# Four column blocks of the first mixing stage computed as two sets of seven block products

## What is computed

```python
h = rmsnorm(x, g_mix[l])
p = h @ w_in[l]                      # 1024 x 5632: F, B, C, V, P (512 each) and three gates of 1024
gates = sigmoid(p[..., OFF_G:]).reshape(b, s, 3, d)
y_f = fourier_mix(p[..., OFF_F:OFF_B], w_fourier[l])
y_c = short_conv(B, C, V, w_conv[l], w_conv_out[l])    # z = C * V, three taps over time, times B, @ w_conv_out
y_p = pool_mix(p[..., OFF_P:OFF_G], w_pool[l], pool_scale[l])
merged = gates[:, :, 0] * y_f + gates[:, :, 1] * y_c + gates[:, :, 2] * y_p
x = x + merged @ w_o[l]
```

## Time and profile before

| | us |
|---|---|
| median of 3 runs (2215.43 to 2217.01) | 2215.58 |
| the profiled execution | 2217.72 |
| its span, first to last instruction | 2215.9 |
| PE busy in the span | 2208.1 |
| DVE busy in the span | 1729.2 |
| ACT busy in the span | 1321.5 |
| mixing stage of the first layer, from about | 188.7 |

### The profile page before, as it was taken

The page is one execution under the profiler, slowest core; times in us unless marked ns, Lnnn a source line. Parts: engine busy times, 40 slices in busy tenths (PEclk is TensorE's granted clock), DMA queues, the critical chain, the costliest instruction groups (busy, mean ns, idle before and its releaser), DMA issues.

```text
span 2215.9 us, 28791 instructions
## 1 busy us (share of the span) xinstructions
PE 2208.1 (100%) x11494; PEld 1886.2 (85%) x11494; DVE 1729.2 (78%) x2163; ACT 1321.5 (60%) x1489; POOL 56.0 (3%) x68
## 2 busy tenths in 40 slices
PE   9999999999999999999999999999999999999999
PEld 8888888888888888888888888888888888788887
DVE  7887566888788566788888799768788887976787
ACT  6566445556556544666656676555565667754555
POOL 0000000000000000000000000000000000000000
PEclk9999999999999999999999999999999999999999
DMA  7977555977879556698597753549778785345876
GB/s 274 327 224 259 166 185 186 310 224 234 287 245 273 187 172 208 215 300 236 193 321 239 236 171 118 204 160 325 231 234 277 239 261 195 105 162 195 287 244 185
DMA packets 170950, 503.86 MB, mean 227 GB/s; under 512 B 18720, under 2 KB 23328, under 8 KB 162624
## 3 DMA queue, kind: packets, MB, share of 16 engines
q1 hardware_dynamic: 161456, 434.90, 55.1%
q0 software_dynamic: 9216, 67.11, 15.4%
q10 hardware_dynamic: 144, 0.00, 0.0%
HBM read 500.91 MB, written 1.05 MB: 227 GB/s over the span
## 4 chain that ended last, share of the span: by engine, by line
PE 90%; DVE 4%; DMA 4%; ACT 1%; issue 1%; SPq 0%; ACTq 0%; DVEq 0%
PE psum L756 24%; PE psum L757 12%; PE psum L692 12%; PE psum L694 12%; PE psum L693 12%; PE psum L888 4%; PE psum L892 4%; PE psum L890 4%; DMA raw<-t_gate_up_1a_dram 2%; DVE split_w L1843 2%; PE psum L724 2%; DMA raw<-t_gate_up_2a_dram 1%; PE psum L1115 1%; DVE gate_up L1983 1%; ACT split_w L1315 0%
## 5 line engine op out<-in xcount | busy, mean ns | idle before, releaser
L1843 DVE TENSOR_TENSOR split_w<-raw,split_w 128x2048 fp32r<-128x2048 f32 (+3 forms) x389 | 842.5, 2177 | 147.4 <-ACT split_w L1315 145.2
L1315 ACT ACTIVATE split_w<-raw 128x2048 fp32r<-128x2048 f32 (+3 forms) x389 | 708.5, 1830 | 291.4 <-PE psum L694 58.4
L756 PE MATMUL psum<-xt,split_w 128*128 128x512 f32 x2464 | 860.1, 393 | 0.5 <-DVE split_w L1843 0.3
L757 PE MATMUL psum<-xt,split_w 128*128 128x256 f32 x2464 | 690.3, 280 | 0.0
L756 PEld LDWEIGHTS psum<-xt,split_w 128*128 128x128 f32 x2464 | 461.2, 187 | 104.0 <-issue 0.6
L757 PEld LDWEIGHTS psum<-xt,split_w 128*128 128x128 f32 x2464 | 465.7, 189 | 0.5
L692 PE MATMUL psum<-split_w,xt 128*128 128x512 f32 (+1 forms) x736 | 289.5, 393 | 0.0
L694 PE MATMUL psum<-split_w,xt 128*128 128x512 f32 (+1 forms) x736 | 283.7, 385 | 0.0
L693 PE MATMUL psum<-split_w,xt 128*128 128x512 f32 (+1 forms) x736 | 283.6, 385 | 0.0
L1983 DVE TENSOR_TENSOR gate_up<-psum,low 128x512 f32<-128x512 f32 x176 | 120.7, 686 | 98.3 <-ACT low L1392 98.1
L692 PEld LDWEIGHTS psum<-split_w,xt 128*128 128x128 f32 x736 | 138.3, 188 | 28.9 <-issue 3.0
(11 more groups left out here) (309 smaller groups left out, 2871.6 us busy)
## 6 DMA issues: line engine op xcount, KB each, us to landing
raw<-w_in_dram SPq DMA_DIRECT2D x180, 512.0 KB, 4.5
raw<-t_gate_up_1b_dram SPq DMA_DIRECT2D x88, 512.0 KB, 6.5
raw<-t_gate_up_2a_dram SPq DMA_DIRECT2D x88, 512.0 KB, 5.9
raw<-t_gate_up_2b_dram SPq DMA_DIRECT2D x88, 512.0 KB, 6.1
raw<-t_gate_up_1a_dram SPq DMA_DIRECT2D x84, 512.0 KB, 6.8
left_sums<-ffn_w_down_quarters_dram POOLq DMA_DIRECT2D x24, 1024.0 KB, 10.0
raw<-ffn_w_down_quarters_dram SPq DMA_DIRECT2D x48, 512.0 KB, 4.4
left_sums<-w_a_quarters_dram POOLq DMA_DIRECT2D x12, 1024.0 KB, 11.0
```

The source lines that it names most:

```text
L756: nc.tensor.matmul(bank, whi[:, slot, w], xt[:, c, :, :], start=c == 0, stop=False)
L757: last = nc.tensor.matmul(bank[:, 0:T], wlo[:, slot, w], xt_hi[:, c, :], start=False, stop=c == DC - 1)
L1315: nc.scalar.activation(whi[:, e.unit(u) % HL, 0:n], raw[:, r, 0:n], ACT.Copy).then_inc(hi_done, 1)
L1843: nc.vector.tensor_tensor(wlo[:, e.unit(u) % HL, 0:n], raw[:, r, 0:n], whi[:, e.unit(u) % HL, 0:n], ALU.subtract).then_inc(w_ready, 1)
```

## The change

The columns C and V are one set (n = 0), and the second halves of the Fourier gate and of the pooling gate are the other (n = 1). For a set, the tokens (two halves) and the depth (even and odd chunks) make the left matrix 2 by 2, and depth and the two column blocks make the right one 2 by 2. In place of two wide products, 96 matmuls, PE computes seven `product`s of 12 matmuls each: 11, U, T2, 21, T3, 22, T4. `w_in_quarters` is a copy of these weights laid out in quarters.

- The sums of token blocks (`s_hi`, `s_lo`, in the space of `mt1`) are made once a layer by `token_sums` and `token_sums_lo` on DVE, with one ACT copy, early in the stage. The three right factors 11, 21 and 22 come through the ring. The four sums come from `set_sums`: POOL issues all their DMAs, the plain loads too. `set_left` holds U, T2 and T4 in turn and `set_right` holds T3, in the space of `poolm`.
- T2 and T3 are added in the bank that holds 11, and 22 in the bank of U. ACT copies the bank away in between (the snapshots `e1`, `u`, `e2`, `e3`), and PE waits for each copy. DVE makes the four output blocks from them (`x00`, `x01`, `x11`, and T4's own bank).
- Order of units now: F, P, B, first half of the Fourier gate, its `t_fourier`, set 0, pooling gate and `w_pool` (n = 0), convolution gate, `w_conv_out`, convolution gate (n = 1), `w_conv_out`, set 1 with `w_pool` inside it ahead of T4, `t_fourier`, `w_o`. There are 38 units, 8 of them sums that do not pass the ring. The merges of the pooling and Fourier branches of n = 1 come after set 1.

```diff
-MIX_UNITS = {1: 32, 2: 36}
+SETS = ({name: 9 + i for i, name in enumerate(("11", "U", "T2", "21", "T3", "22", "T4"))},
+        {"11": 25, "U": 26, "T2": 27, "21": 28, "T3": 29, "22": 30, "T4": 32})
+SET_SUMS = [units[name] for units in SETS for name in ("U", "T2", "T3", "T4")]
+SUMMED = {"U": 0, "T3": 1, "T2": 2, "22": 3}
+MIX_UNITS = {1: 38, 2: 36}
...
+        s_hi, s_lo = (w.rearrange("p (i a) (b t) -> p i (a b) t", a=2, b=2) for w in (mt1_hi, mt1_lo))
...
+        def bank_of(name):
+
+            return 2 if name == "21" else 1 if name in ("U", "22") else 0
...
+                def product(n, name):
+                    out = psum[:, bank_of(name), :]
+                    u = u0 + set_unit(n, name)
+                    slot = e.unit(u) % HL
+                    eng.wait_ge(w_ready, units(e, u, RAW))
+                    for i in range(DC // 2):
+                        hi, lo = left(name, i)
+                        w = slice(i * 512, (i + 1) * 512)
+                        start = i == 0 and name in ("11", "U", "21")
+                        stop = i == DC // 2 - 1
+                        nc.tensor.matmul(out, hi, whi[:, slot, w], start=start, stop=False, skip_group_check=True)
+                        nc.tensor.matmul(out, hi, wlo[:, slot, w], start=False, stop=False, skip_group_check=True)
+                        last = nc.tensor.matmul(out, lo, whi[:, slot, w], start=False, stop=stop, skip_group_check=True)
+                    last.then_inc(w_used, 1)
+
+                wide(u0 + 6, 1, XT)
+                eng.wait_ge(acted, e.after(acted, ("tok", "B")))
+                branch_out(u0 + 8, 2, (fq_hi, fq_lo), 0)
+
+                product(0, "11")
+                eng.wait_ge(done, e.after(done, ("s",)))
+                product(0, "U")
+                eng.wait_ge(acted, e.after(acted, ("e1", 0)))
+                product(0, "T2")
+                eng.wait_ge(acted, e.after(acted, ("sig", 0, "f")))
+                product(0, "21")
+                eng.wait_ge(acted, e.after(acted, ("e2", 0)))
+                product(0, "T3")
+                eng.wait_ge(acted, e.after(acted, ("u", 0)))
+                product(0, "22")
+                eng.wait_ge(acted, e.after(acted, ("e3", 0)))
+                product(0, "T4")
...
+                product(1, "11")
+                product(1, "U")
+                eng.wait_ge(acted, e.after(acted, ("e1", 1)))
+                product(1, "T2")
+                eng.wait_ge(acted, e.after(acted, ("sig", 1, "c")))
+                product(1, "21")
+                eng.wait_ge(acted, e.after(acted, ("e2", 1)))
+                product(1, "T3")
+                eng.wait_ge(acted, e.after(acted, ("u", 1)))
+                product(1, "22")
+                turns("mt0", ptok)
+                eng.wait_ge(done, e.after(done, ("merged", 1, "c")))
+                branch_out(u0 + 31, 2, (pl_hi, pl_lo), 1)
+                eng.wait_ge(acted, e.after(acted, ("e3", 1)))
+                product(1, "T4")
+                eng.wait_ge(done, e.after(done, ("x00", 1)))
+                branch_out(u0 + 33, 1, (fq_hi, fq_lo), 1)
+                u = u0 + 34
+
+                eng.wait_ge(done, e.after(done, ("mt0", 1)))
+                eng.wait_ge(done, e.after(done, ("x01", 1)))
                 eng.wait_ge(acted, e.after(acted, ("sig", 1, "f")))
-                wide(u, 0, XT)
-                eng.wait_ge(done, e.after(done, ("merged", 1, "p")))
-                blocks(u + 2, 0, 2, (bz_hi, bz_lo), range(4), True, True, True)
-                u += 3
-
-                eng.wait_ge(done, e.after(done, ("mt0", 1)))
-                eng.wait_ge(acted, e.after(acted, ("sig", 1, "c")))
                 wide(u, 0, MERGED, 0, 1)
                 blocks(u, 2, 0, MERGED, (2,), False, False, False)
-                eng.wait_ge(done, e.after(done, ("merged", 1, "c")))
+                eng.wait_ge(done, e.after(done, ("merged", 1, "f")))
                 turns("mt1", merged1)
...
+                set_sum_split(0, "U")
...
+                gate(0, "f", 1, u0 + 7)
+                set_sum_split(0, "T2")
+                split(u0 + 12)
+                snapshot("e1", 0, "11", z[:, 0, :])
+                set_sum_split(0, "T3")
+                snapshot("u", 0, "U", sigs[:, 1, 1, :])
+                split(u0 + 14)
+                snapshot("e2", 0, "T2", sigs[:, 1, 0, :])
+                set_sum_split(0, "T4")
+                split(u0 + 16)
+                snapshot("e3", 0, "T3", sigs[:, 0, 1, :])
+                split(u0 + 17)
...
+                set_sum_split(1, "T2")
+                split(u0 + 28)
+
+                snapshot("e1", 1, "11", sigs[:, 0, 0, :])
+                set_sum_split(1, "T3")
+                snapshot("u", 1, "U", sigs[:, 1, 1, :])
+                split(u0 + 30)
+                snapshot("e2", 1, "T2", sigs[:, 1, 0, :])
+                split(u0 + 31)
+                set_sum_split(1, "T4")
+                snapshot("e3", 1, "T3", sigs[:, 0, 1, :])
+                eng.wait_ge(done, e.after(done, ("wf", 1)))
+                split(u0 + 33)
+                eng.wait_ge(done, e.after(done, ("x00", 1)))
+                sigmoid(sigs[:, 0, 0, :], sigs[:, 0, 0, :], 0)
+                eng.wait_ge(done, e.after(done, ("x11", 1)))
+                sigmoid(sigs[:, 1, 1, :], sigs[:, 1, 1, :], 1)
+                eng.wait_ge(done, e.after(done, ("x01", 1)))
+                sigmoid(sigs[:, 1, 0, :], sigs[:, 1, 0, :], 0).then_inc(acted, e.mark(acted, ("sig", 1, "p")))
+                for j in range(2):
+                    turned_hi(mt1_hi, ("mt0", j), 6 + j, 2 * j)
+                split(u0 + 34)
+                split(u0 + 35)
+                multiplied(u0 + set_unit(1, "T4"))
+                sigmoid(sigs[:, 0, 1, :], psum[:, bank_of("T4"), :], 1).then_inc(
+                    acted, e.mark(acted, ("sig", 1, "f")))
+                split(u0 + 36)
...
+            def set_sums(u0):
+
+                def load(out, q, n, semaphore):
+                    eng.dma_start(out[:, :], set_quarter(e, q, n)).then_inc(semaphore, 16)
+                    eng.wait_ge(semaphore, 16 * (set_turn(e, n) + 1))
+
+                def add(out, q, n, semaphore):
+                    eng.dma_start(out[:, :], set_quarter(e, q, n), accum_op=ALU.add).then_inc(semaphore, 16)
+
+                def split_done(n, name):
+                    eng.wait_ge(w_ready, units(e, u0 + set_unit(n, name), RAW))
+
+                for n in range(2):
+                    if n == 0:
+                        eng.wait_ge(done, e.after(done, ("s",)))
+                    else:
+                        split_done(0, "T4")
+                    load(set_left, "11", n, set_left_in)
+                    add(set_left, "12", n, set_left_added)
+                    if n == 0:
+                        eng.wait_ge(small, e.after(small, ("pl", 1)))
+                    load(set_right, "12", n, set_right_in)
+                    add(set_right, "22", n, set_right_added)
+                    split_done(n, "U")
+                    eng.wait_ge(set_left_added, 16 * (3 * set_turn(e, n) + 1))
+                    add(set_left, "22", n, set_left_added)
+                    split_done(n, "T2")
+                    eng.wait_ge(set_left_added, 16 * (3 * set_turn(e, n) + 2))
+                    add(set_left, "21", n, set_left_added)
...
+                e.link(nc.vector.tensor_tensor(flat.rearrange("p (c t) -> p c t", c=DC), xt_hi, xt_lo, ALU.add))
+                q = flat.rearrange("p (i k t) -> p i k t", k=4, t=P)
+                sa = set_left.rearrange("p (i k t) -> p i k t", k=4, t=P)
+                e.link(nc.vector.tensor_tensor(sa[:, :, 0:2, :], q[:, :, 3:1:-1, :], q[:, :, 1::2, :], ALU.subtract))
+                e.link(nc.vector.tensor_tensor(sa[:, :, 2, :], sa[:, :, 0, :], q[:, :, 2, :], ALU.subtract))
+                nc.vector.tensor_tensor(sa[:, :, 3, :], sa[:, :, 2, :], q[:, :, 0, :], ALU.add).then_inc(
+                    done, e.mark(done, ("sa",)))
...
+                set_sum_split(0, "T2")
+                split(u0 + 12)
+                set_sum_split(0, "T3")
+                split(u0 + 14)
+                quarter_added(0, z[:, 0, :])
+                set_sum_split(0, "T4")
+                split(u0 + 16)
+                snapshots_apart(0)
+                split(u0 + 17)
+                quarter_apart(0)
+                eng.wait_ge(done, e.after(done, ("x01", 0)))
+                nc.vector.scalar_tensor_tensor(out=z[:, 0, :], in0=sigs[:, 1, 0, :], scalar=rstd_squared[:, 0:1],
+                                               in1=z[:, 0, :], op0=ALU.mult, op1=ALU.mult).then_inc(
+                                                   done, e.mark(done, ("z", 0)))
+                split(u0 + 18)
+                multiplied(u0 + set_unit(0, "T4"))
+                nc.vector.scalar_tensor_tensor(out=z[:, 1, :], in0=sigs[:, 1, 1, :], scalar=rstd_squared[:, 1:2],
```

(25 more changed lines are left out.)

334 lines of the change are left out of this document (197 added, 137 removed).

## The result

The changed kernel takes **2263.28 us** (median of 4 runs, 2260.37 to 2264.28) beside 2216.3 us for the kernel before on the same chip: a ratio of 1.0209, 95% interval 1.0191 to 1.0226. It is 47.0 us slower. Forecast were 2257 us, 41.5 slower, with a range of 2240 to 2269.

A forecast was written before the change was run, and what follows sets the result against it. PE's matmul count was taken to bound the kernel, busy 2208.1 of 2215.9 us. Stalls of 52.4 us over two layers, less 10.9 saved, gave 2215.6 + 41.5 = 2257 us, range 2240 to 2269.

The forecast's parts named there:

- The saving: Two sets in each of two layers: 84 matmuls for 96, 48 fewer in all, 10.9 us (0.49%) gained.
- The additions: POOL's 1 MB additions: 11 us for T2's in set 0, 8.7 for T4's, 8 for T2's in set 1.
- Set 0: First set of a layer: PE stalls of 8.1 us at T2, 2.6 at T4 and 2.3 at z.
- the clock rival: Clock falls to 1.2 GHz in stalls; only 24 slow matmuls after a layer's last stall cost, 5.4 us: 2268 us; chance 0.15.
- gates and conv products give everything slack: After z in set 0: no further PE stall claimed before set 1.
- Set 1: Second set of a layer: PE stalls of 1.1 us at T2, 0.9 at block 21 and 0.7 at T4.
- The tail: From T4 of set 1: stalls of 4.6 us at first w_o product, 5.2 at merged transposes, 0.7 behind: 10.5 a layer.
- The walk: Step-by-step timing of the chains PE waits for, through set 0, set 1 and the tail: 26.2 us of stalls a layer.
- The sum: Stalls of 13.0 + 2.7 + 10.5 = 26.2 us a layer, 52.4 for both, less 10.9: +41.5 us.
- The prediction's own sign: PE idle of about 26 us in each of the two mixing stages, the largest at T2 of set 0.
- Fast additions: Rival: additions land in 4 to 5 us, T2's first stall about 2, 12.5 us a layer, 2230 us; chance 0.11.
- The covered tail: Rival: ACT and DVE finish in time, the tail's 10.5 us vanishes, with fast additions 2210 us; chance 0.03.

The follow-up runs named there:

- the filled run: Changed kernel plus overwritten matmuls ahead of T2 of set 0, the first w_o product and the transposes of merged, keeping PE busy through long waits: 2262.81 us.
- first experiment: Changed kernel, but ACT and DVE split the ready token sums in place of the four sums, so no split waits for an addition: 2227.58 us.

## Why the prediction was right, point by point

**The saving**, 10.9 us: right in the stages (5.1 and 4.8 of 5.4 each); the medians show 7.8, with 10.9 inside their interval.

**The additions.** I took 11 us for T2's in set 0; they took 12.4 and 10.6 in the two layers. For T4's and those of set 1, 8.7, 8 and 8.7 were taken, and 8.3, 7.9 and 8.2 measured in layer 1 (9.8, 7.9 and 8.3 in layer 2). The rows of before had this between the first and second of a pair, and for T2 the place in the queue made the difference, as the run with the addition ahead shows. That a first addition takes 7.7 to 9.0 was not so for U's (11.6 to 12.2), which the sum did not need.

**Set 0**, forecast 8.1 at T2, 2.6 at T4 and 2.3 at z. Measured in layer 1: 9.2, none, 1.5 and 1.0 at `bz`; in layer 2: 7.4, 0.9 and 1.9. T4's stall is filled by slow matmuls, as the clock rival's working had it and the filled run shows; with the slow matmuls counted I estimate some 14 us of loss in each layer from the steps of the trace, for 13.0 forecast. That "gates and conv products give everything slack" was wrong by the 1.0 at `bz`.

**Set 1**, forecast 1.1, 0.9 and 0.7. Measured: 0.9 and 0.7 in layer 1 (0.8 and 0.7 in layer 2), and nothing at T4.

**The tail**, forecast 4.6, then 5.2 and 0.7. Measured 3.8 and 3.9 at the first product, right in place. The walk had DVE's split of that unit done at 8.6 and the sigmoid at 8.8, and they end at 351.1 and 351.2 us; but the prediction names the sigmoid alone as the cause, which is only half of it. At the transposes 1.9 and 3.1, with some 14 and 8 slow matmuls ahead of them filling the rest. With the clock up the wait is 4.8 (first experiment).

**The sum.** Forecast 26.2 us of stalls a layer, less 5.4: +20.8. Measured +22.0 and +21.3, of which the idle time is 18.9 and 19.1 only. The mechanism and the size of the sum were right, and the kind was partly another: between a quarter and a third of it shows as slow matmuls and transposes, not as waiting. The prediction's own sign, PE idle of about 26 us in each stage, is so missed by 7 us. Of the 5.5 us by which the total was missed, 1.7 lie in the two stages and 1.5 in the rest of the profiled execution, which the forecast had at nothing; by 2.2 the medians of the runs lie further apart than the profiled spans.

**The rivals.** Fast additions (4 to 5 us): no addition was that fast. The nearest to it are the runs with half the bytes (5.2 to 6.4 us for T2's and T4's) and with plain copies (5.0 to 6.0), both 2235, for 2230 worked out. The clock rival: the clock did fall, against my sum's silence on it, but the 24 slow matmuls behind the last wait of a layer, its 5.4 us, were some 6 and slow transposes in layer 1 and none in layer 2, and each cost 0.20 us, not 0.227; filling the waits gained nothing. The covered tail: with the tail's waits and those for additions gone together the kernel is 7.8 us faster than before, with only the latter gone 11 slower. No run covers the tail alone; by these steps, in which it brings 19 of 55 us, that would not have made the kernel faster.
